# One launch, first layer and start: order of the first transfers, rotary angles beside the first projections, stick-breaking heads in pairs

## What is computed

```
SEQ, D_MODEL, DEPTH, SB_HEADS, HEAD_DIM = 256, 1024, 2, 8, 64

def _stick_breaking_attention(q, k, v):          # first branch, 8 heads of 64
    z = jnp.einsum('bthd,bshd->bhts', q, k) * scale
    strict = s_idx[None, :] < t_idx[:, None]
    log_beta = jax.nn.log_sigmoid(z)
    log_1m = jnp.where(strict, jax.nn.log_sigmoid(-z), 0.0)
    later = lax.cumsum(log_1m, axis=3, reverse=True) - log_1m
    w = jnp.where(strict, jnp.exp(log_beta + later), 0.0)
    return jnp.einsum('bhts,bshd->bthd', w, v)

def _partial_rope(x, positions):                 # third branch: cos and sin of the positions
    ang = positions[:, :, None] * inv_freq
    cos, sin = jnp.cos(ang), jnp.sin(ang)
    ...

def _layer(x, ...):
    h = _rmsnorm(x, g_mix)
    proj = h @ w_in                              # (qa, ka, va) first, then the others, then gates
    br_a = _stick_breaking_attention(qa, ka, va)
    log_f = jax.nn.log_sigmoid(fl + b_forget)    # second branch
    br_b = _forgetting_attention(qb, kb, vb, log_f)
    br_c = _indexed_sparse_attention(...)        # with _partial_rope on its inputs
    y = gates[0] * (br_a @ w_branch[0]) + gates[1] * (br_b @ w_branch[1]) + gates[2] * (br_c @ w_branch[2])
    ...
```

## Time and profile before

| what | value |
|---|---|
| time, median of 3 runs | 2830.69 us (2826.34 to 2836.09) |
| the profiled execution's own time | 2839.29 us |
| its span (first to last instruction) | 2837.5 us |
| instructions | 34393 |
| busy: PE, DVE, ACT, POOL | 92%, 62%, 48%, 3% of the span |
| mean granted TensorE clock | 0.943 |

### The profile page before, as it was taken

How to read it: one execution, slowest core, us unless ns; L and a number is a source line. 1 busy time by engine, 2 the same in 40 slices (tenths; PEclk the granted TensorE clock), 3 DMA queues, 4 the chain that set the end, 5 groups by cost and what they waited for, 6 DMA issues and landing times. The chain is left out here.

```text
span 2837.5 us, 34393 instructions
## 1 busy us (share of the span) xinstructions
PE 2597.4 (92%) x13657; PEld 2120.2 (75%) x13657; DVE 1751.7 (62%) x2022; ACT 1363.3 (48%) x1501; POOL 93.3 (3%) x146
## 2 busy tenths in 40 slices
PE   4899889998999899976889989799999999999996
PEld 4695459886954699845879977687877888787785
DVE  3332445553434455565564454688888888888887
ACT  2631224446312244422234344477777777777775
POOL 0100010001000100003200000000000000000000
PEclk9997999999989999987989985799999999999998
DMA  7250244542412445430065531599999999999996
GB/s 269 83 178 30 89 156 179 178 156 94 178 59 89 157 178 178 135 64 12 2 223 178 187 104 60 196 368 357 358 344 362 355 346 362 351 360 344 363 355 229
DMA packets 391567, 586.56 MB, mean 207 GB/s; under 512 B 21169, under 2 KB 284657, under 8 KB 391281
## 3 DMA queue, kind: packets, MB, share of 16 engines
q1 hardware_dynamic: 391408, 584.37, 60.5%
HBM read 580.13 MB, written 4.19 MB: 206 GB/s over the span
## 5 line engine op out<-in xcount | busy, mean ns | idle before, releaser
L2889 DVE TENSOR_TENSOR moe_low<-ring,moe_high 128x2048 fp32r<-128x2048 f32 x288 | 658.1, 2289 | 107.1 <-ACT moe_high L2853 104.7
L2853 ACT CAST moe_high<-ring 128x2048 fp32r<-128x2048 f32 x288 | 550.6, 1912 | 168.4 <-PE bank L2790 88.1
L2784 PE MATMUL bank<-moe_high,moe_xh 128*128 128x512 f32 x896 | 240.7, 391 | 7.9 <-PEq L2609 7.9
L2784 PE MATMUL bank<-moe_high,moe_xl 128*128 128x512 f32 x896 | 240.4, 390 | 0.0
L2784 PE MATMUL bank<-moe_low,moe_xh 128*128 128x512 f32 x896 | 240.1, 390 | 0.0
L2784 PEld LDWEIGHTS bank<-moe_high,moe_xh 128*128 128x128 f32 x896 | 168.5, 188 | 43.3 <-issue 8.1
L2784 PEld LDWEIGHTS bank<-moe_high,moe_xl 128*128 128x128 f32 x896 | 168.8, 188 | 35.3
L2784 PEld LDWEIGHTS bank<-moe_low,moe_xh 128*128 128x128 f32 x896 | 168.6, 188 | 35.1
L1620 DVE TENSOR_TENSOR chain_low<-upper_ring,chain_high 128x2048 fp32r<-128x2048 f32 x36 | 82.5, 2292 | 97.6 <-ACT chain_high L1594 97.6
L2790 PE MATMUL bank<-moe_high,moe_hh 128*128 128x512 f32 x448 | 127.5, 406 | 15.2 <-DVE moe_hl L2894 8.0
L1594 ACT CAST chain_high<-upper_ring 128x2048 fp32r<-128x2048 f32 x36 | 68.5, 1903 | 120.9 <-PE bank L1565 61.9
(11 more groups left out here) (490 smaller groups left out, 4915.1 us busy)
## 6 DMA issues: line engine op xcount, KB each, us to landing
ring<-in_moe_w_gate SPq DMA_DIRECT2D x206, 512.0 KB, 5.1
ring<-in_moe_w_up SPq DMA_DIRECT2D x206, 512.0 KB, 6.7
ring<-in_moe_w_down SPq DMA_DIRECT2D x88, 1024.0 KB, 7.2
ring<-in_w_in SPq DMA_DIRECT2D x18, 2048.0 KB, 8.1
xT<-in_moe_w_down SPq DMA_DIRECT2D x25, 1024.0 KB, 6.9
upper_ring<-in_w_in SPq DMA_DIRECT2D x10, 2048.0 KB, 8.0
upper_ring<-in_w_up SPq DMA_DIRECT2D x10, 2048.0 KB, 8.0
upper_ring<-in_w_down SPq DMA_DIRECT2D x8, 2048.0 KB, 8.0
```

Source lines behind the costliest of these rows:

```text
L2784: mm = pe.matmul(core.banks[i % 2][:], (xl if other_low else xh)[:, place(m), 4 * part + c, :], wt[:, c, :], start=(part == 0 and j == 0 a ...
L2853: act.copy(unit(high, u), ring.raw(u)).then_inc(s["weight_high"], 1)
L2889: dve.tensor_tensor(unit(low, u), ring.raw(u), unit(high, u), ALU.subtract)\
```

## The change

1. `start_stage` issues `x`, the norm's gain, the constants and weight tile 0, in this order, and waits for `x` and the constants only.
2. The stage of the angles is gone. Its loads and those of the biases and the six small vectors are issued in `norm_stage`, behind weight tile 1 (`small_loads`). Its 13 DVE instructions stand in the first projections behind the fifth unit, its two ACT instructions (and their table load) behind ACT's last store there. The stage that uses the biases waits for them by a semaphore of their own.
3. Of the ring's fill, tiles 2 to 5 are issued at the start of the first projections (`before=... w.fill(sp, 2)`), not in the norm's stage.
4. `stick_stage` takes heads two at a time. Everything elementwise on DVE, ACT and the tiles behind it is 768 columns wide where it was 384 (the copies out of PSUM and the differences, which read banks, stay one to a head). Four steps of pairs replace eight of heads, and the gates' ten steps are dealt out as (0, 1), (2, 3), (4), (5, 6), (7, 8), (9), the second of each behind the sums.

```diff
-            for i in range(H + 2):
...
+            for i in range(PAIRS + 2):
+                n = i
+                if n < PAIRS:
+                    if n:
+                        pe.wait_ge(s["kept"], 2 * n)
+                    for h, _ in heads(n):
...
+                logits.step(pe, steps[i][0])
...
+                for step in steps[i][1:]:
+                    logits.step(pe, step)
...
-                logits.store_between(dve, i)
...
+                if i == 3:
+                    logits.store(dve, 0)
...
                 if i == 0:
-                    norm_stage(core, norm, lead, w.fill)
+                    angles = Angles(core, a["positions"], core.cos, core.sin, core.angle_room)
+
+                    def small_loads(sp):
+                        w.load(sp, 1)
+                        angles.load(sp)
+                        for j in range(DEPTH):
+                            sp.dma_start(core.b_forget[:, j, :], row_broadcast(a["b_forget"][j])).then_inc(core.bias_there, 16)
+                        core.band.load(sp)
+                    norm_stage(core, norm, lead, small_loads)
...
-                        (base + 2, "N", BW, keep_N(core, v))], norm, 4)
+                        (base + 2, "N", BW, keep_N(core, v))], norm, 4,
+                        before=None if i else lambda sp: w.fill(sp, 2), angles=None if i else angles)
...
-def start_stage(core, a):
+def start_stage(core, a, w):
...
+            sp.dma_start(core.x[:], a["x"].rearrange("o (t p) d -> p (o t) d", p=P)).then_inc(loaded, 16)
+            core.affine.fetch(sp, "mix0")
             sp.dma_start(core.consts[:], a["consts"]).then_inc(loaded, 16)
...
-            sp.wait_ge(loaded, 16 * (2 + DEPTH))
+            w.load(sp, 0)
+            sp.wait_ge(loaded, 16 * 2)
```

More of the change, by code:

```diff
@@ L643, in pair, with split_projection_stage @@
     return core.banks[2 * (n % 2)], core.banks[2 * (n % 2) + 1]
-def split_projection_stage(core, tag, w, jobs, x=None, first_bank=0, before=None, beside=None):
+def split_projection_stage(core, tag, w, jobs, x=None, first_bank=0, before=None, beside=None, angles=None):
     nc = core.nc
@@ L796, in _ @@
                         x.keep(act, u - 4)
+                if angles is not None:
+                    angles.act(act)
             @block.vector
@@ L816, in _ @@
                             x.low(dve, b)
+                    if u == 4 and angles is not None:
+                        angles.dve(dve)
 def copy(eng, core, out, in_):
@@ L1143, in _ @@
         def _(act):
[L1144 to L1159 removed]
+            for i in range(PAIRS + 1):
+                n = i
+                if n < PAIRS:
+                    if n >= 2:
+                        act.wait_ge(s["diff"], 2 * n - 2)
+                    for h, c in heads(n):
+                        act.wait_ge(s["scores"], h + 1)
+                        act.copy(z[:, n % 2, c:c + TRI], core.banks[h % 2][:, 0:TRI]).then_inc(s["kept"], 1)
+                    act.wait_ge(s["minus_abs"], n + 1)
+                    act.activation(small[:, n % 2, :], small[:, n % 2, :], ACT.Exp).then_inc(s["exp"], 1)
+                    act.wait_ge(s["exp"], n + 1)
+                    act.activation(small[:, n % 2, :], small[:, n % 2, :], ACT.Ln, bias=1.0).then_inc(s["log"], 1)
+                n = i - 1
+                if n >= 0:
+                    act.wait_ge(s["diff"], 2 * n + 2)
+                    act.activation(w[:, n % 2, :], w[:, n % 2, :], ACT.Exp).then_inc(s["weights"], 1)
+            act.wait_ge(s["summed"], PAIRS)
             act.copy(out[:, 1, :], core.banks[5][:])
@@ new lines, with __init__, load, dve @@
+class Angles:
+    def __init__(self, core, positions, cos, sin, tmp):
+        self.core, self.positions, self.cos, self.sin = core, positions, cos, sin
+        self.s = {n: core.sem(f"angle_{n}") for n in ("loaded", "step", "done")}
+        self.pos = tmp[:, 0:2].bitcast(I32)
+        self.posf = tmp[:, 2:4]
+        self.ang = tmp[:, 4:20].rearrange("p (t f) -> p t f", t=NT)
+        self.turns = tmp[:, 20:36].rearrange("p (t f) -> p t f", t=NT)
+    def load(self, sp):
+        sp.dma_start(self.pos, self.positions.rearrange("o (t p) -> p (o t)", p=P), allow_slow_non_contiguous=True)\
+          .then_inc(self.s["loaded"], 16)
+    def dve(self, dve):
+        s, pos, posf, ang, turns, cos, sin, core = (self.s, self.pos, self.posf, self.ang, self.turns, self.cos, self.sin,
+                                                    self.core)
+        two_pi = (6.28125, 0.0019350051879882812, 3.019915981956753e-07)
+        step = [0]
+        def then(op):
+            op.then_inc(s["step"], 1)
+            step[0] += 1
+            dve.wait_ge(s["step"], step[0])
+        dve.wait_ge(s["loaded"], 16)
+        then(dve.tensor_copy(posf, pos))
+        for t in range(NT):
+            then(dve.tensor_scalar(ang[:, t, :], core.const("freq"), posf[:, t:t + 1], None, ALU.mult))
+        then(dve.tensor_scalar(turns, ang, 1.0 / (2.0 * np.pi), 12582912.0, ALU.mult, ALU.add))
+        then(dve.tensor_scalar(turns, turns, 12582912.0, None, ALU.subtract))
+        for c in two_pi:
+            then(dve.scalar_tensor_tensor(out=ang, in0=turns, scalar=-c, in1=ang, op0=ALU.mult, op1=ALU.add))
+        then(dve.tensor_scalar(sin, ang, np.pi - 1e-6, -np.pi + 1e-6, ALU.min, ALU.max))
+        then(dve.tensor_scalar(ang, ang, np.pi / 2, None, ALU.add))
+        then(dve.tensor_scalar(turns, ang, np.pi, -2.0 * np.pi, ALU.is_gt, ALU.mult))
+        then(dve.tensor_tensor(ang, ang, turns, ALU.add))
+        dve.tensor_scalar(cos, ang, np.pi - 1e-6, -np.pi + 1e-6, ALU.min, ALU.max).then_inc(s["done"], 1)
+    def act(self, act):
+        act.wait_ge(self.s["done"], 1)
+        act.activation(self.sin, self.sin, ACT.Sin)
+        act.activation(self.cos, self.cos, ACT.Sin)
@@ L1810, in build @@
         core.b_forget = core.sbuf("b_forget", [P, DEPTH, KC])
+        core.bias_there = core.sem("bias_there")
+        core.angle_room = core.sbuf("angle_room", [P, 36])
         core.affine = Affine(core, a)
         core.band = Band(core, a)
-        start_stage(core, a)
-        with core.scratch("start"):
-            tmp, _ = core.part(0, 36)
-            angles_stage(core, a["positions"], core.cos, core.sin, tmp)
         r = moe_small(core)
```

187 lines of the change are left out of this document (66 added, 121 removed).

## The result

The changed kernel takes 2800.49 us (median of 4 runs, 2798.81 to 2811.52), the kernel before 2833.14 us (median of 4, 2826.34 to 2836.09). The ratio is 0.9889 with an interval of 0.9866 to 0.9911: faster by 1.1%, between 0.9 and 1.3. The forecast was 2807 us with a range of 2798 to 2818.

What follows compares the result with a forecast made beforehand. SyncE's transfer list was taken to bound the norm's stage, TensorE's own work the stick-breaking stage. Terms -19.3 + 1.6 - 6.3 = -24.0 us gave 2815.3 against the profile, 2807 against the median; range 2798 to 2818.

Steps and rivals of the forecast that it cites:

- What bounds: First block: engines idle for SyncE's issues at the norm's stage, not for bandwidth; TensorE's own work bounds the stick-breaking stage.
- Norm's start: Start stage: with the new order of transfers the norm starts at 10.9 us instead of 17.0, 6.1 earlier.
- Start of the projections: End of the norm's stage, set by SyncE's list: projections start at 24.3 us, 19.3 earlier; bounds 20.9 and 28.
- rival (a): Norm's stage: SyncE is not held, projections start at 20.9, 3.4 us less, 2803 us; chance 0.2.
- (b): Norm's stage: SyncE is held longer, projections start at 28, 2811 us; chance 0.12.
- Fill beside the projections: First projections: tiles 2 to 5 land before they are asked for, 0 us, with 17 us of margin.
- Angles on DVE: First projections, behind the fifth unit: 2.8 us of DVE work, costing 0 us by a margin of 0.3, at worst 0.5.
- Sine and cosine: ACT behind the last store of the first projections: table load and instructions add 1.6 us on the path, once.
- rival (e): Stick-breaking stages: TensorE starves once in each of four pair steps per layer, with lower clock behind; 2847 us; chance 0.04.
- Pairs: Stick-breaking stage: TensorE's work stays 47.8 us, each layer's stage takes 48.8; gains 4.2 and 2.1, together 6.3 us.
- Rival (c): Stick-breaking stage: the pairs give nothing because TensorE waits at the store as before; 2813 us; chance 0.1.
- (d): First projections: they start earlier only to wait for tiles 1 and 2; 2820 to 2826 us; chance 0.07.

Runs made afterwards that it cites:

- the start alone: The changed kernel with the stick-breaking stage of the kernel before, all else as changed: 2820.75 us, ratio 0.9956.
- one half of the rows: The changed kernel with queries and keys of every head read from partitions 0 to 63: 2809.79 us in one run.
- the products: Three matmuls with unused results added in TensorE's idle time ahead of the second branch: kernel before 2827.33 us, pairs alone 2813.22.
- the two with both moves: The changed kernel with small transfers behind tile 2 and sine and cosine inside the first projections: 2802.06 us; with three extra products 2793.69.

## Why the prediction was right, and where it was not

Its sum was -24.0 us against the profile; the profile shows -27.7. The median came a further 2.4 us lower, because the profiled run lies 11.0 above its median and not 8.6.

- **What bounds.** Right. The norm's stage was ended by SyncE's list, and the run with the fill put back shows 16.5 of the 20.6 us there. Nothing later had to give any of it back to transfers: ahead of the second layer's stage the difference is 24.6, more than behind the first layer's.
- **Norm's start.** Forecast 10.9, measured 11.46. What came later than estimated are the constants, issued at 1.82 and landed 9.2 us later at 11.0, not 10.5. The gain ahead of them landed at 1.31 + 6.2 = 7.5, which is 1.5 us behind `x` (0.81 + 5.2) and not 1.3; whether the rest comes of weight tile 0, issued right behind them, is not shown (DMA issues, 0 to 62 us: count, KB, median us to landing):

```profile
consts<-in_consts SPq DMA_DIRECT2D x1, 1416.0 KB, 9.2
x<-in_x SPq DMA_DIRECT2D x1, 1024.0 KB, 5.2
affine_rows<-in_g_mix SPq DMA_DIRECT2D x1, 512.0 KB, 6.2
```

- **Start of the projections.** Forecast 24.3, measured 22.96. That SyncE is held by the small transfers, and that this ends the stage, was right: the run with them moved away takes the hold out (start 21.18), so it was not rival (a), in which SyncE is never held; (b) fell too. The size was worked out wrongly. It stood on "tile 1's landing + 2.0", 23.3. SyncE came free at 21.4, and tile 1, issued at 11.42, landed only at 21.9 (the same view for 11 to 12 us):

```profile
ring<-in_w_in SPq DMA_DIRECT2D x1, 2048.0 KB, 10.5
```

So no landing set SyncE free, and that the two times lie 1.3 us apart is in part luck. The forecast's other reading, room for about 2,000 pieces, does better. The traces have every piece as a packet, with 16 more for the semaphore of each transfer. So the count per transfer that the forecast missed is there: in the first 17 us of before, the packets of 4 bytes are 1,728, which is 1,024 + 256 + 256 for the transfers read element by element and 16 for each of 12 semaphores. I counted those issued and not yet moved when each transfer of the first 62 us was issued, in all twelve traces: with 1,855 or fewer waiting none held SyncE over 1.4 us, with over 2,170 all but one (1.04) held it 2.6 to 7.5 us, and in between both occur. The small transfer that held it 3.98 us here had 2,623 ahead of it, that of before (2.74 us) 2,003.
- **Fill beside the projections.** Right, 0 us: from 63.23 back to 22.96 are 40.3 us, where 82.43 - 43.60 = 38.8 stood before, and the difference of 1.4 is the sine's.
- **Angles on DVE.** They begin at 37.09, where 57.87 - 20.6 = 37.3 was due, and end at 39.88: 2.8 us as forecast. The 1.4 us of the last point are the whole growth of that stretch, so they cost TensorE nothing.
- **Sine and cosine.** Forecast 1.6 us, measured 1.5 (TensorE's idle time ahead of the scores grew from 1.05 to 2.55). By the drain that "ScalarE: Activation LUTs" of the Trainium skill, section "What ACT_TABLE_LOAD costs", adds it would have been 3.0; the sine starts at 62.62, 0.02 behind the load's end, and the trace decides against it here. But the step stopped too early: it priced the wait and not what follows a wait. Behind 2.55 us of idle time the granted clock averaged 0.73 over 63 to 75 us, so it was partly at 1.2 GHz, and 3.05 us more were lost. All five kernels with 2.55 us of idle at that place show the slow stretch right behind it (the changed one, the start alone, the small transfers moved, one half of the rows, the fill put back); with 1.05 us (the kernel before and the pairs alone, each with and without the products, sine and cosine moved, and the two with both moves) none does. The forecast had such a fall in its rival (e), priced at a wait of 1.94, and did not carry it to the one wait that it added itself.
- **Pairs.** Forecast 6.3 us (4.2 and 2.1), measured 10.7 (4.9 and 5.8). Where the slow stretch ahead of it is gone, the first layer's stage takes 45.1 us too, which is 7.9 less than before. The step that failed is "TensorE's work stays 47.8", and with it the 48.8 us. In the second layer, where no slow stretch disturbs, the stage takes 45.1. The 5.8 us less: the wait for the store fell from 1.52 to 0.17, 1.35; the overlap of two heads in two halves, 2.3; what a pair's scores cost even without it, 4 x 1.50 against 8 x 0.84, 0.7. That leaves 1.4. Adding up the distances between TensorE's starts by kind of work finds 1.2 of it. The outputs take 6.12 us instead of 6.87, because a pair's and no longer one head's stand behind the last gate logits, where VectorE's last stores end the stage anyway (2.17 us from the start of these outputs to the stage's end, 2.09 before with half as many). The gate logits take 28.16 instead of 28.48, the sums 7.14 instead of 7.22. What remains lies in the scores' own distances. The margin at the store was forecast at 1 us, but TensorE came at 22.7 us into the stage and not at 25.8, and waited 0.17. The row of before for the store there:

```profile
679.23 2.81 PE L901 MATMUL bank<-upper_ring,xT 128*128 128x512 f32 x6 [1.52 <-DVE lower_arena L913]
```

- **Rival (c)**, the pairs give nothing: wrong in place, and yet what the total of the run with the pairs alone shows (1.000). The total alone would have seemed to confirm it.
- **Rivals (d) and (e)**: no sign. TensorE never waits for a sum; the widened operations took 0.96 (DVE) and 0.84 us (ACT), as estimated. After, grouped by line and shape, first layer's stage (busy us, mean ns, idle before):

```profile
L1136 DVE SCALAR_TENSOR_TENSOR upper_a_arena<-upper_a_arena 128x768 f32<-128x768 f32 x4 | 3.8, 959 | 10.3 <-ACT upper_a_arena L1167 10.3
...
L1169 ACT ACTIVATE upper_a_arena<-upper_a_arena 128x768 f32<-128x768 f32 x4 | 3.4, 842 | 2.3 <-DVE upper_a_arena L1136 2.3
```

- **What was not in it at all:** the granted clock in stretches that the change doesn't touch. It moved 3.8 us against the change in its profile at about 1262, and some 11 us one way or the other in other kernels. That the number came out so near owes something to this: start and pairs brought 1.3 and 4.4 us more than forecast, which would be -29.8; the 3.8 lost, and 1.6 gained in small steps elsewhere, make -27.7 of it.

What stays open: by what, besides TensorE's idle time just ahead, the second branch gets full or half clock. It differs between the two layers of one run. That the clusters of the run times are clock is on record: each run has its mean granted clock, and for the kernel before it is 0.946 to 0.948 near 2826.5 us, 0.945 or 0.946 near 2830.7, 0.944 near 2835.5 and 0.943 near 2838.5. The lost share times the span, 0.053 x 2825 = 150 us and 0.057 x 2837 = 162 (the third digit is worth 3 us), differs by the 12 us between the outer clusters. In the changed kernel it is 0.941 at 2811.52 us and 0.944 or 0.945 at the three runs near 2800. Which stretch the lost clock lies in is recorded only for the profiled runs, so that it is the second branch is not shown; with the extra products there the kernel before fell mostly within 2825.4 to 2829.3, which fits.

## What to carry to other kernels

Where a stage ends with a barrier, the list of the engine that issues transfers counts as work: put into it what the stage needs and nothing that can be issued behind the barrier, and keep transfers of many small pieces out of it. Price a wait that you add on TensorE together with the clock behind it, and look for other work in its gap, or move what causes it to where another engine is waiting anyway. And judge an edit by the shift of its own place between two traces as well as by the total: here stretches of lower clock some 100 us further on hid 11.5 of 15 us of gain.

## What was not expected of the hardware

- Matmuls of 64 rows in the two halves of the partitions overlap when they stand next to each other in TensorE's queue: two heads' scores in 0.86 us against 1.50 in one half.
- After 2.55 us of idle on TensorE the next 9 us ran partly at half clock in five kernels of five; after 1.05 us in none. Where TensorE idled 3.5 us ahead of it, the second branch began with some 17 or some 31 us at half clock, and which of them it was changed with edits 100 us earlier; the difference is worth some 11 us.
- SyncE issued six small transfers in 4.75 us, one of them of 1,024 single elements, and was then held 4.66 us by the next two, of 128 single elements each. Neither bytes nor the number of transfers gives that; the number of pieces waiting to be moved fits it, as it fitted: in twelve traces no hold over 1.4 us began with 1,855 or fewer waiting, and all over 2,170 but one were such holds.
